# SyncE issues the value pages of the last two samples, and GpSimd's squares in the first layer's output projections stand between two weight splits

## The chip, the cores and the metric

The kernel runs on one core of a Trainium2 chip. Five engines run their own streams and wait for each other on semaphores: TensorE (matrix products), VectorE, ScalarE, GpSimd and SyncE, which here only issues transfers. The metric is the device time of one execution in microseconds; lower is better. Three runs of the kernel before gave 1976.70, 1977.17 and 1978.89 us, a median of 1977.17.

## The reference

One inference step of a decoder with two layers, for a prompt of 1024 tokens and for 8 samples of 8 new tokens each (64 tokens), with a width of 1024, in float32. All 1088 tokens share the weights. Cut to what matters here:

```python
# layer 0: gated MLP over chunks
u, v, z = split(rmsnorm(x) @ w_in_a, 3)
x = x + (u * spatial_mix(rmsnorm(v)) * silu(z)) @ w_out_a      # 2048 -> 1024
# layer 1: sparse attention, 8 query heads, 2 key/value heads of 128
q, k, v, iq, ik, iw, z = split(rmsnorm(x) @ w_in_b)
idx = top_k(indexer_scores(iq, iw, ik_all), 256)               # per query token
x = x + (softmax(q @ k_sel) @ v_sel * silu(z)) @ w_out_b       # k_sel, v_sel: chosen positions
# after each layer
x = x + sigmoid(rmsnorm(x) @ w_gate) * (p @ w_pe)
```

A sample attends to 1024 past positions. Their keys and values lie in pools of pages of 128 positions, and page_table names the 8 pages of each sample: for each sample 8 pages of keys and 8 of values, 128 KB each, have to be fetched by number.

## The kernel before

**Activations and weights.** Activations are kept transposed, with channels on the partitions: xT is 8 tiles of 128 channels by 1092 columns (64 sample tokens, 1024 prompt tokens, 4 of padding). Weights come in 177 units of 1024 x 128 (512 KB). Each matrix product in full precision is made of three products of rounded parts: hi x hi, hi x lo, lo x hi. So each unit goes through four steps, and with two buffers (par 0 and 1, in turn) for each: SyncE loads wraw (unit, L602), ScalarE rounds it to whi (split_hi, L429) once TensorE has used the unit two before, GpSimd computes wlo = wraw - whi (split_lo, L434), and TensorE waits for w_lo and runs the unit (gemm, L446); w_used counts the units that it has left.

**Output projections of the first layer.** The first layer runs over two token groups, one after the other: 576 columns, then 512. In a group, w_out_a makes 8 tiles of output channels, each of two units (half 0 and half 1). When TensorE leaves a tile, VectorE adds it to xT (L1423) and raises xup. GpSimd then adds the squares of that tile to acc (add_squares: the square L759, the sum L760), for the norm that follows; for tile 7 that is left to ScalarE. In the order of GpSimd's stream the squares of tile f stand right behind the two splits of turn f, which are unit 2f + 1 and unit 2f + 2 of the projection; the next turn's first split, of unit 2f + 3, is behind them. From tile 3 of the second group on, VectorE also makes the low parts that the gate needs (gate_lo, L493) right behind L1423.

**Sample attention.** It follows the prompt attention in the second layer. TensorE goes through the samples with a lead: for each b it transposes the probabilities of b (sample_turn), folds sample b - 1 (L2500), makes the logits of b + 2, transposes the keys of b + 3 (k_pages, L2442) and multiplies the probabilities of b with its values (sample_values: L2485 for the new tokens, L2489 for the pages). Key and value pages have three buffers each, kpg and vpg, taken in turn by b % 3. SyncE issues key pages (key_pages): those of samples 0 to 2 early, those of 3 to 7 when the keys of b - 3 have been transposed (sa["kt"]). GpSimd issues value pages: samples 0 to 2 during the prompt attention, then eight loads of z tiles, then samples 3 to 7, each when the product of sample b - 3 is done (sa["pv"]). Each issue (sample_pages, L589) reads a page number into a register and starts one transfer; the transfers of sample b raise vpin[b % 3], or kpin[b % 3] for keys, by 16 each. Behind its last value page GpSimd clears acc (L855) and makes the low part of unit 162, the second of w_out_b. Behind its last key page SyncE waits for the last sample's output and then reloads xT from DRAM (L713).

**Behind it.** VectorE copies the last sample out (L1894), multiplies it with the gate z (L1873), ScalarE rounds it (L1282), VectorE takes the low part (L1938), and TensorE starts the output projection of the second layer.

Of the kernel before, what the change touches and what calls it, by code (L numbers as in the profile page):

```python
# [28 lines left out]
KD = D // P  # L29
SEQ, DEC_B, DEC_T = 1024, 8, 8  # L30
# [7 lines left out]
KA = AW // P  # L38
# [4 lines left out]
PAGE, NPAGE = 128, 8  # L43
# [14 lines left out]
U_A = [0, 64]  # L58
# [5 lines left out]
def tile_cols(j):  # L64

    return (0, NS) if j == 0 else (NS + CHUNK * (j - 1), CHUNK)
# [52 lines left out]
def hybrid_trunk(nc, x_prompt, x_sample, cache_k, cache_v, cache_ik, page_table, p_prompt, p_sample,  # L119
# [5 lines left out]
    with ctx:  # L125
        def sem(name):
            return ctx.enter_context(nc.semaphore(name))
# [60 lines left out]
        sqa = rbc  # L188
# [83 lines left out]
        vpg = [pl(f"vpg{q}", [P, NPAGE, NKV * DH]) for q in range(2)]  # L272
        vpg = [[t[:, 0:NPAGE // 2], t[:, NPAGE // 2:]] for t in vpg]
# [67 lines left out]
        sA = [Turn(gmlp, {n: g * {"vsq": 5, "rv": 1, "xup": KD}.get(n, KA) for n in gmlp}) for g in range(2)]  # L341
# [50 lines left out]
        sa = {n: sem(f"sa_{n}") for n in ("pre", "qc", "kt", "ke", "s", "mx", "nb", "ex", "nr", "tr", "pt", "pv", "hd", "ft", "o")}  # L392
        kpin, vpin = ([sem(f"{n}{q}") for q in range(3)] for n in ("kpin", "vpin"))
# [10 lines left out]
        for n, (b, h) in enumerate(STEPS):  # L404
# [3 lines left out]
            PIECES += [(n, b, h, m) for m in range((b + 4) // 4)]  # L408
        SPREAD_AT = [FIRST[n] - 1 for n in SPREAD] + [len(PIECES)]
        LAST = [FIRST[n] + (b + 4) // 4 for n, (b, _) in enumerate(STEPS)]  # L410
        FRONT = ((2, 0), (3, 0))
        SCORES = ([(b, c, h) for b, c in FRONT for h in range(IH - 2)] +
# [18 lines left out]
        def split_lo(pool, par, u):  # L431

            pool.wait_ge(w_hi, u + 1)
            nc.gpsimd.tensor_tensor(wlo[par][:], wraw[par][:], whi[par][:].bitcast(F32),  # L434
                                    ALU.subtract).then_inc(w_lo, 1)
# [136 lines left out]
        def group_cols(g):  # L572
            c0, n, _, _, np_ = GROUPS[g]
            return [(c0 + n // np_ * m, n // np_) for m in range(np_)]
# [9 lines left out]
        def sample_pages(eng, dst, src, b, done, pages=range(NPAGE)):  # L584

            for g in pages:
                page = eng.value_load(ptab[0:1, b * NPAGE + g:b * NPAGE + g + 1],
                                      min_val=0, max_val=cache_k.shape[0] - 1)
                eng.dma_start(dst(g), src[bass.ds(page, 1), 0].rearrange("a s g d -> s (a g d)")).then_inc(done, 16)  # L589

        def value_pages(pool, b, pages=range(NPAGE)):
            if b >= 3:
                pool.wait_ge(sa["pv"], b - 2)
            sample_pages(pool, lambda g: vpg[b % 3][g // 4][:, g % 4, :], cache_v, b, vpin[b % 3], pages)

        @block.sync
        def _(sp):
# [14 lines left out]
            for j in range(9):  # L612
                c0, n = tile_cols(j)
# [87 lines left out]
            def key_pages(b):  # L701
                if b >= 3:
                    sp.wait_ge(sa["kt"], b - 2)
                sample_pages(sp, lambda g: kpg[b % 3][:, g, :], cache_k, b, kpin[b % 3])
# [4 lines left out]
                key_pages(b)  # L709
            for b in range(3, DEC_B):  # L710
                key_pages(b)
            sp.wait_ge(sa["o"], DEC_B)
            sp.dma_start(xT[:].rearrange("p f n -> p (f n)"), xs).then_inc(xs_in, 16)  # L713
            sp.wait_ge(oy["lo"], KD)
# [10 lines left out]
        def _(pool):  # L725
# [31 lines left out]
            def add_squares(sq, f, a, n):  # L757

                own.link(nc.gpsimd.tensor_tensor(sq, xT[:, f, a:a + n], xT[:, f, a:a + n], ALU.mult))  # L759
                own.link(nc.gpsimd.tensor_tensor(acc[:, a:a + n], acc[:, a:a + n], sq, ALU.add))  # L760

            for g in range(2):
                c0, n, _, _, np_ = GROUPS[g]
                for base, trips in ((U_A[g], KA // 2), (U_A[g] + KA, KA)):
                    with pool.Fori(0, trips) as i:
                        for ff in range(2):
                            split_lo(pool, (ff + 1) % 2, base + 2 * i + ff + 1)
                    if base == 0:
                        pool.wait_ge(ws_ev, 2)
                        own.link(nc.gpsimd.affine_select(out=wsT[:], in_=wsT[:], compare_op=ALU.is_ge, fill=0.0, base=0,  # L770
                                                         pattern=[[0, NGRP], [1, P]], channel_multiplier=-1))
                        for b in range(DEC_B):
                            t = slice(DEC_T * b, DEC_T * b + DEC_T)
                            pool.dma_start(wsbd[t, :, t], wsT[0:DEC_T, :, 0:DEC_T]).then_inc(bd_in, 16)
                pool.wait_ge(nA[g]["sum"], nA[g].at("sum", np_))
                own.link(nc.gpsimd.memset(acc[:, c0:c0 + n], 0.0))
                for f in range(KD):
                    for half in range(2):
                        split_lo(pool, (half + 1) % 2, U_A[g] + 3 * KA + 2 * f + half + 1)
                    if f < KD - 1:  # L780
                        pool.wait_ge(sA[g]["xup"], sA[g].at("xup", f + 3))
                        add_squares(sqa[:, c0:c0 + n], f, c0, n)
                pool.sem_inc(stat, 1)

            def gate_pool(layer, last):
# [53 lines left out]
            for i in range(NBLK * NKV):  # L839
                pool.wait_ge(at_["rs"], i + 1)  # L840
                if i:
                    pool.wait_ge(at_["tr"], SPREAD_AT[i - 1] + 1)
                nc.gpsimd.tensor_tensor(rdiag[:], ident[:].unsqueeze(1).broadcast_to((P, REP, P)),
                                        ars[:, REP * i:REP * i + REP].unsqueeze(2).broadcast_to((P, REP, P)),
                                        ALU.mult).then_inc(at_["dg"], 1)
                if 1 <= i <= 6:
                    value_pages(pool, (i - 1) // 2, range(4 * ((i - 1) % 2), 4 * ((i - 1) % 2) + 4))
# [2 lines left out]
                pool.wait_ge(z_st[q], 16 * (KD // 2))  # L850
            for f in range(KD):
                pool.dma_start(zb[f][:], zs[f]).then_inc(z_in[f // 2], 16)
            for b in range(3, DEC_B):
                value_pages(pool, b)
            own.link(nc.gpsimd.memset(acc[:], 0.0))  # L855
            for f in range(KD):
# [9 lines left out]
        def _(act):  # L866
# [349 lines left out]
            def pieces_out(n):  # L1216
                for i in range(FIRST[n], LAST[n]):
                    _, b, h, m = PIECES[i]
                    k = min(4, b + 1 - 4 * m)
                    act.wait_ge(at_["tr"], i + 1)  # L1220
                    if n >= REP:
                        act.wait_ge(at_["pv"], n // 2 - 1)
                    nc.scalar.activation(PTs[:, 4 * m:4 * m + k, h % REP, :],
                                         PS[:, 4 + i % 2, 0:k * P].rearrange("p (k q) -> p k q", q=P),
                                         ACT.Copy).then_inc(at_["pt"], 1)
# [726 lines left out]
        def _(pe):  # L1952
# [19 lines left out]
            for g in range(2):  # L1972
                c0, n, nch, has_s, np_ = GROUPS[g]
# [57 lines left out]
                with pe.Fori(0, KA // 2) as i:  # L2031
                    for ff in range(2):
                        f = 2 * i + ff
# [195 lines left out]
            for m, (b, c, h) in enumerate(SCORES):  # L2229
                n = min(BANK, (b + 1) * P - c * BANK)  # L2230
                p0 = ID * (h % 2)
                c0 = tile_cols(1 + b)[0]
# [244 lines left out]

            def sample_values(b):
                pe.wait_ge(sa["pt"], b + 1)
                pe.wait_ge(vpin[b % 3], 16 * NPAGE * (b // 3 + 1))  # L2480
                if b:
                    pe.wait_ge(sa["hd"], b)
                tiles = [(q, g, PS[NS * q + 32 * g:NS * q + 32 * g + 32, 3, 0:P]) for q in range(2) for g in range(NKV)]
                for g in range(NKV):
                    nc.tensor.matmul(tiles[g][2], PsT[0:NS, 8, 32 * g:32 * g + 32], vtok[0:NS, 0, g * DH:(g + 1) * DH],  # L2485
                                     start=True, stop=False)
                for j in range(NPAGE // 2):
                    for q, g, out in tiles:
                        mm = nc.tensor.matmul(out, PsT[:, 2 * j + q, 32 * g:32 * g + 32],  # L2489
                                              vpg[b % 3][q][:, j, g * DH:(g + 1) * DH], start=q == 1 and j == 0,  # L2490
                                              stop=j == NPAGE // 2 - 1)
                mm.then_inc(sa["pv"], 1)
# [15 lines left out]
            for b in range(DEC_B):  # L2508
                sample_turn(b)
                if b:  # L2510
                    fold_halves(b - 1)
                if b + 2 < DEC_B:
                    sample_logits(b + 2)
                if b + 3 < DEC_B:
                    k_pages(b + 3)
                sample_values(b)
# [32 lines left out]
```

## Time and profile before

| | |
|---|---|
| median of three runs | 1977.17 us (1976.70 to 1978.89) |
| span of the profiled execution | 1973.8 us |
| its own time | the page gives the span alone; the median of the runs is 3.4 us above it |
| TensorE busy | 1863.0 us, 94% |
| VectorE, ScalarE, GpSimd busy | 862.2, 793.2, 649.9 us |
| DMA | 150.76 MB, mean 76 GB/s |

A busy TensorE doesn't mean TensorE at its peak: its clock has two levels, 2.4 and 1.2 GHz, and PEclk in a row is the mean granted one as a share of the upper. Rows in order of time give the start in us from the start of the span, the duration, the engine and line, what is written and read, the count of instructions merged in the row, and in brackets how long the engine stood idle before and what ended that. "issue" stands for time in which the profile shows nothing that the engine waited for. POOL is GpSimd, DVE is VectorE, ACT is ScalarE, PE is TensorE, PEld its weight loads, SPq SyncE's issues.

### The profile page before, as it was taken

The page shows a single profiled execution, that of the slowest core. Times are in us where ns is not written, and L with a number is a line of the kernel's source. Part 1 is how long each engine was busy: PE and PEld are TensorE (multiplying, and loading weights), DVE is VectorE, ACT ScalarE, POOL GpSimd, SP SyncE. Part 2 cuts the span into 40 slices and gives each one's busy share as a digit, 9 for nine tenths or more (in the row PEclk, how much of TensorE's full clock was granted, in tenths as well). Part 3 has the DMA queues.
Part 4 walks back from the last instruction along what each step waited for, and adds up shares of the span by engine and source line. Part 5 has one row for each costly group of instructions (what it writes and reads, how often), then busy time and mean ns, then how long its engine had stood idle before and what let it go on. Part 6 is the DMA issues. An engine that isn't in the chain of part 4 may idle for free. (4 is left out here: it accounts for less than half of the span.)

```text
span 1973.8 us, 30722 instructions
## 1 busy us (share of the span) xinstructions
PE 1863.0 (94%) x11000; PEld 1647.2 (83%) x11000; DVE 862.2 (44%) x1653; ACT 793.2 (40%) x1148; POOL 649.9 (33%) x397
## 2 busy tenths in 40 slices
PE   7999999899999999999979989999989998699998
PEld 7999999899887888779969549999966765499997
DVE  4113333311114444033254877687778634512433
ACT  4233333212243333233235675567865554402211
POOL 4333323265333334654522131111132002354220
PEclk9999999999999999999989899999999999899999
DMA  6223222222222222331123110312231006531111
GB/s 187 75 65 85 74 74 74 64 77 83 85 85 85 85 85 86 95 109 33 32 64 122 31 56 22 89 43 66 88 121 31 1 1 209 186 99 43 44 55 45
DMA packets 226179, 150.76 MB, mean 76 GB/s; under 512 B 16754, under 2 KB 219250, under 8 KB 225714
## 3 DMA queue, kind: packets, MB, share of 16 engines
q1 hardware_dynamic: 210754, 125.78, 21.6%
q0 software_dynamic: 5152, 14.48, 2.4%
q10 hardware_dynamic: 10192, 9.46, 1.4%
q8 instruction: 46, 0.75, 0.2%
q14 instruction: 35, 0.29, 0.1%
HBM read 133.24 MB, written 16.43 MB: 76 GB/s over the span
## 5 line engine op out<-in xcount | busy, mean ns | idle before, releaser
L434 POOL TENSOR_TENSOR wlo<-wraw,whi 128x1024 fp32r<-128x1024 f32 x177 | 430.2, 2431 | 722.4 <-ACT whi L429 720.3
L446 PE MATMUL PS<-hhi_g,whi 128*128 128x288 f32 (+1 forms) x1152 | 324.0, 335 | 12.2 <-POOL wlo L434 7.2
L429 ACT ACTIVATE whi<-wraw 128x1024 fp32r<-128x1024 f32 x177 | 186.6, 1055 | 343.0 <-PE PS L446 324.6
L446 PE MATMUL PS<-hhi_g,wlo 128*128 128x288 f32 (+1 forms) x1152 | 317.1, 330 | 0.0
L446 PE MATMUL PS<-hlo_g,whi 128*128 128x288 f32 (+1 forms) x1152 | 316.9, 329 | 0.0
L446 PE MATMUL PS<-hhi,whi 128*128 128x364 f32 x1176 | 269.7, 338 | 12.8 <-DVE hlo L559 6.8
L446 PE MATMUL PS<-hlo,whi 128*128 128x364 f32 x1176 | 262.0, 331 | 0.0
L446 PE MATMUL PS<-hhi,wlo 128*128 128x364 f32 x1176 | 260.6, 330 | 0.0
L446 PEld LDWEIGHTS PS<-hhi_g,whi 128*128 128x128 f32 x1152 | 195.7, 189 | 31.1 <-issue 6.6
L446 PEld LDWEIGHTS PS<-hhi,whi 128*128 128x128 f32 x1176 | 204.0, 191 | 20.4 <-issue 13.9
L446 PEld LDWEIGHTS PS<-hhi_g,wlo 128*128 128x128 f32 x1152 | 196.4, 189 | 17.7
L446 PEld LDWEIGHTS PS<-hlo_g,whi 128*128 128x128 f32 x1152 | 196.9, 190 | 16.2
L446 PEld LDWEIGHTS PS<-hlo,whi 128*128 128x128 f32 x1176 | 206.5, 190 | 0.0
L446 PEld LDWEIGHTS PS<-hhi,wlo 128*128 128x128 f32 x1176 | 206.3, 190 | 0.0
L446 PE MATMUL PS<-yhi,whi 128*128 128x288 f32 (+1 forms) x384 | 108.0, 335 | 5.3 <-POOL wlo L434 4.7
L1387 DVE TENSOR_TENSOR t2a<-PS,szt 128x576 f32<-128x576 f32 (+1 forms) x32 | 23.2, 725 | 198.9 <-PE PS L446 198.3
L446 PE MATMUL PS<-yhi,wlo 128*128 128x288 f32 (+1 forms) x384 | 106.0, 330 | 0.0
L446 PE MATMUL PS<-ylo,whi 128*128 128x288 f32 (+1 forms) x384 | 105.3, 329 | 0.0
L1626 DVE TENSOR_SCALAR_CACHE_REDUCE acc<-sc,thr 128x384 bf16<-128x384 f32 (+1 forms) x124 | 100.7, 812 | 4.1
L1344 DVE COPY v_raw<-PS 128x512 f32 x32 | 22.1, 691 | 176.7 <-PE PS L1998 91.2
L988 ACT ACTIVATE sig<-hfb 128x1092 f32<-128x1092 f32 x16 | 17.9, 1118 | 174.7 <-DVE hfb L1441 174.5
L1423 DVE TENSOR_TENSOR xT<-PS,xT 128x576 f32<-128x576 f32 (+1 forms) x16 | 11.6, 725 | 168.0 <-PE PS L446 168.0
(392 smaller groups left out, 2726.4 us busy)
## 6 DMA issues: line engine op xcount, KB each, us to landing
wraw<-in_w_in_a_dram SPq DMA_DIRECT2D x96, 512.0 KB, 3.9
wraw<-in_w_out_a_dram SPq DMA_DIRECT2D x32, 512.0 KB, 4.0
wraw<-in_w_in_b_dram SPq DMA_DIRECT2D x25, 512.0 KB, 3.7
wraw<-in_w_pe_gate_dram SPq DMA_DIRECT2D x16, 512.0 KB, 4.2
kpg<-in_cache_k_dram SPq DMA_DIRECT2D x64, 128.0 KB, 2.8
vpg<-in_cache_v_dram POOLq DMA_DIRECT2D x64, 128.0 KB, 2.4
xs<-xT SPq DMA_DIRECT2D x1, 4368.0 KB, 12.6
xT<-xs SPq DMA_DIRECT2D x1, 4368.0 KB, 14.0
```

Of the source, the lines that this page charges most:

```text
L429: nc.scalar.activation(whi[par][:], wraw[par][:], ACT.Copy).then_inc(w_hi, 1)
L434: nc.gpsimd.tensor_tensor(wlo[par][:], wraw[par][:], whi[par][:].bitcast(F32), ALU.subtract).then_inc(w_lo, 1)
L446: mm = nc.tensor.matmul(o, w[par][:, k, :], r(k, c0, cn), start=first and i == 0 and n == 0, stop=last and i == KD - 1 and n == 2)
L988: nc.scalar.activation(sig[:], tg, ACT.Sigmoid).then_inc(s["sig"], 1)
L1344: vdst = nc.vector.tensor_copy(v_raw[:, bass.ds(f, 1), 0:4 * P].rearrange("p o n -> p (o n)"), PS[:, 4 + 2 * ff, :])
L1387: nc.vector.tensor_tensor(t2a[:, 0:n].rearrange("p (b n) -> p b n", b=np_), PS[:, 2:2 + np_, 0:h], szt[:, 0:n].rearrange("p (b n) -> p b n ...
L1423: nc.vector.tensor_tensor(x, PS[:, b:b + np_, 0:h], x, ALU.add).then_inc(s["xup"], 1)
L1626: own.link(nc.vector.tensor_scalar(vdmp[:, 0:(b + 1) * P], area(b), thr[:, b - 2:b - 1], None, ALU.is_lt, ALU.add, accum_out=cnt[:, b - 2: ...
```

## The change

Three things. The value pages of samples 6 and 7 are issued by SyncE, behind its last key pages, and no longer by GpSimd; each still waits for the product of sample b - 3. Their transfers raise a semaphore of the key pages (the one that the keys of sample b - 1 had used), so value_sem(b) tells both the issuer and TensorE which semaphore and which count it is. And in the output projections of the first layer the squares of tile f - 1 stand in GpSimd's stream between the two splits of turn f, where the squares of tile f stood behind both. The number of squares, splits and transfers is the same.

```diff
+        def value_sem(b):
+            if b < DEC_B - 2:
+                return vpin[b % 3], 16 * NPAGE * (b // 3 + 1)
+            q = (b - 1) % 3
+            return kpin[q], 16 * NPAGE * ((DEC_B - 1 - q) // 3 + 2)
-        def value_pages(pool, b, pages=range(NPAGE)):
+        def value_pages(eng, b, pages=range(NPAGE)):
             if b >= 3:
-                pool.wait_ge(sa["pv"], b - 2)
-            sample_pages(pool, lambda g: vpg[b % 3][g // 4][:, g % 4, :], cache_v, b, vpin[b % 3], pages)
+                eng.wait_ge(sa["pv"], b - 2)
+            sample_pages(eng, lambda g: vpg[b % 3][g // 4][:, g % 4, :], cache_v, b, value_sem(b)[0], pages)
...
             for b in range(3, DEC_B):
                 key_pages(b)
+            for b in range(DEC_B - 2, DEC_B):
+                value_pages(sp, b)
             sp.wait_ge(sa["o"], DEC_B)
...
                 for f in range(KD):
-                    for half in range(2):
-                        split_lo(pool, (half + 1) % 2, U_A[g] + 3 * KA + 2 * f + half + 1)
-                    if f < KD - 1:
-                        pool.wait_ge(sA[g]["xup"], sA[g].at("xup", f + 3))
-                        add_squares(sqa[:, c0:c0 + n], f, c0, n)
+                    split_lo(pool, 1, U_A[g] + 3 * KA + 2 * f + 1)
+                    if f:
+                        pool.wait_ge(sA[g]["xup"], sA[g].at("xup", f + 2))
+                        add_squares(sqa[:, c0:c0 + n], f - 1, c0, n)
+                    split_lo(pool, 0, U_A[g] + 3 * KA + 2 * f + 2)
...
-            for b in range(3, DEC_B):
+            for b in range(3, DEC_B - 2):
                 value_pages(pool, b)
...
-                pe.wait_ge(vpin[b % 3], 16 * NPAGE * (b // 3 + 1))
+                pe.wait_ge(*value_sem(b))
```

## Rows read from the trace of the kernel before

**Rows 1.** The page: busy time and share of the span.
```profile
PE 1863.0 (94%) x11000; PEld 1647.2 (83%) x11000; DVE 862.2 (44%) x1653; ACT 793.2 (40%) x1148; POOL 649.9 (33%) x397
```

**Rows 2.** Groups of TensorE, 376 to 486 and 776 to 884: busy, mean, idle before.
```profile
L446 PE MATMUL PS<-yhi,whi 128*128 128x288 f32 x256 | 56.5, 301 | 0.3
...
L446 PE MATMUL PS<-yhi,whi 128*128 128x512 f32 x128 | 51.5, 402 | 5.1 <-POOL wlo L434 4.7
```

**Rows 3.** TensorE in order of time, 1630 to 1730.
```profile
1636.25 1.97 PE L2442 MATMUL PS<-ident,kpg 128*128 128x128 f32 x16
...
1683.22 1.08 PE L2489 MATMUL PS<-vpg,PsT 128*32 128x128 f32 x32
...
1696.22 0.41 PE L2485 MATMUL PS<-vtok,PsT 64*32 64x128 f32 x4
...
1697.57 0.66 PE L2475 MATMUL PS<-ident,Ps 128*128 128x128 f32 x4
...
1702.52 0.41 PE L2485 MATMUL PS<-vtok,PsT 64*32 64x128 f32 x4 [3.26 <-issue]
...
1712.11 0.64 PE L2485 MATMUL PS<-vtok,PsT 64*32 64x128 f32 x4 [5.53 <-issue]
...
1715.02 0.69 PE L2500 MATMUL PS<-rsb 128*128 128x64 f32 x2 [0.41 <-DVE rsb L1890]
1718.92 1.25 PE L446 MATMUL PS<-hhi,whi 128*128 128x364 f32 x3 [3.21 <-DVE hlo L1938]
```

**Rows 4.** GpSimd's issues of value pages in order of time; landing, 1680 to 1711.
```profile
1690.63 0.54 POOL L589 DMA_DIRECT2D vpg<-in_cache_v_dram  x1 [0.61 <-issue]
...
1709.63 0.54 POOL L589 DMA_DIRECT2D vpg<-in_cache_v_dram  x1 [0.61 <-issue]
...
DMA to landing us min/median/max: 2.2/2.3/3.4
```

**Rows 5.** SyncE's issues in order of time; landing of key pages, 1674 to 1684.
```profile
1638.96 44.02 SPq L589 DMA_DIRECT2D kpg<-in_cache_k_dram  x40
1716.00 0.33 SPq L713 DMA_DIRECT2D xT<-xs  x1
...
DMA to landing us min/median/max: 2.8/3.1/3.9
```

**Rows 6.** All engines in order of time around the last sample.
```profile
1700.15 0.21 ACT L1271 ACTIVATE PsT<-PS 64x64 f32<-64x64 f32 x1
...
1710.16 1.03 POOL L855 MEMSET acc<- 128x1092 f32 x1
1711.27 2.34 POOL L434 TENSOR_TENSOR wlo<-wraw,whi 128x1024 fp32r<-128x1024 f32 x1
...
1716.01 0.36 DVE L1873 TENSOR_TENSOR qT<-qT,zb 128x64 f32<-128x64 f32 x2
```

**Rows 7.** Windows: busy per engine, granted clock, DMA share, GB/s.
```profile
core 0: us, PE busy (x) PEld busy (x) DVE busy (x) ACT busy (x) POOL busy (x), PEclk, DMA share, GB/s
1703.10:1706.50 3.40, 3.40 (x39) 2.50 (x31) 0.29 (x1) 0.39 (x1) 1.54 (x4) 0.52 0.40 102
...
1718.90:1723.50 4.60, 4.58 (x15) 4.60 (x16) 4.60 (x8) 3.87 (x4) 0.00 (x0) 0.51 1.07 463
```

**Rows 8.** Second group's output projection, in order of time, 782 to 880.
```profile
791.69 0.69 DVE L1423 TENSOR_TENSOR xT<-PS,xT 128x512 f32<-128x512 f32 x1 [6.18 <-PE PS L446]
...
792.47 1.04 POOL L759 TENSOR_TENSOR rbc<-xT 128x512 f32<-128x512 f32 x1 [2.78 <-DVE xT L1423]
793.58 1.29 POOL L760 TENSOR_TENSOR acc<-acc,rbc 128x512 f32<-128x512 f32 x1
...
826.52 0.69 DVE L1423 TENSOR_TENSOR xT<-PS,xT 128x512 f32<-128x512 f32 x1 [10.92 <-PE PS L446]
826.58 1.07 ACT L429 ACTIVATE whi<-wraw 128x1024 fp32r<-128x1024 f32 x1 [3.86 <-PE PS L446]
827.13 1.35 DVE L493 SCALAR_TENSOR_TENSOR hlo<-xT,gp,hhi 128x1092 fp32r<-128x1092 f32 x1
827.29 2.08 POOL L759 TENSOR_TENSOR rbc<-xT 128x512 f32<-128x512 f32 x1 [3.19 <-DVE xT L1423]
...
830.82 4.90 POOL L434 TENSOR_TENSOR wlo<-wraw,whi 128x1024 fp32r<-128x1024 f32 x2
...
877.04 0.69 DVE L1423 TENSOR_TENSOR xT<-PS,xT 128x512 f32<-128x512 f32 x1 [10.69 <-PE PS L446]
```

## The prediction, made before the result was known

> **What bounds the kernel now.** Five views, in this order. The page first: TensorE is busy for 1863.0 of the 1973.8 us of the span, and no other engine for half of it [rows 1], so a change pays only where TensorE waits or runs at its lower clock. Then the groups of instructions over the two output projections of the first layer: TensorE's matmuls there stand idle 0.3 us in the first token group and 5.1 us in the second, 4.7 of it put down to GpSimd's low parts (L434) [rows 2]. Then TensorE in order of time through the sample attention, where it waits 3.26 us and 5.53 us in front of the value products of samples 6 and 7 [rows 3]. Then GpSimd's and SyncE's issues in the same stretch: which queue is late [rows 4, 5]. Last, the windows, for the clock granted around these waits [rows 7].
>
> The profiled execution has a span of 1973.8 us; the median of the three runs is 1977.17, that is 3.4 more for what lies around the span. I work on the span and take the difference off the median. What this kernel's measurement can tell from no change is about 0.2%, 4 us.
>
> **Part one: value pages of samples 6 and 7 on SyncE.** GpSimd issues samples 3 to 7 in one row: the last page of sample 5 starts at 1690.63, the last of sample 7 at 1709.63, 16 pages later, 1.19 us each with the gaps; a page lands 2.3 us after its issue (median) [rows 4]. So sample 7 lands at about 1711.9, and TensorE starts on it at 1712.11. The waits follow from GpSimd's pace of issue.
>
> SyncE is not quicker: 40 key pages take 44.02 us from the first start to the last end, (44.02 - 0.33) / 39 = 1.12 us a page (the 0.33 is one issue, as in the row of its reload) [rows 5]. But it ends with the keys at 1682.98 and then stands idle until 1716.00. What gates the moved pages:
> - sample 6 overwrites the buffer of sample 3, whose product ends at 1683.22 + 1.08 = 1684.30 [rows 3]. From a release to SyncE's first issue take 0.74 us: the first transposes of keys end at 1636.25 + 1.97 = 1638.22, SyncE starts at 1638.96 [rows 3, 5]. First page 1685.04.
> - sample 7 waits for the product of sample 4, which lies about halfway between that of sample 3 and that of sample 5 (1696.22) [rows 3], near 1692; SyncE has its eight pages for sample 6 out only at 1694.0, so it doesn't wait.
> - 15 more pages: last issue 1685.04 + 15 x 1.12 = 1701.84. Landing took between 2.8 and 3.9 us on this queue while both queues were full, 2.2 at the shortest and 3.4 at the longest on GpSimd's [rows 4, 5]. By then only one queue issues, so I take 2.4: 1704.3 (1703.9 to 1705.7).
>
> Sample 6's pages land by 1696 and no longer count. Its product then waits for ScalarE's copy of the probabilities, which ends at 1700.15 + 0.21 = 1700.36 [rows 6]: it starts at 1700.45 and not at 1702.52. Sample 7 by computation: product 1.35 us at the full clock (1696.22 to 1697.57, where the next group of matmuls starts), transposes 0.9, ScalarE's copy 0.8: ready at 1703.5. The pages, at 1704.3, are the later of the two. Start moves from 1712.11 to 1704.3: **7.8 us** (6.4 to 8.2; computation alone would give 8.6).
>
> After it, before: 2.91 us from the start of the product to the fold (1715.02), at half clock; at the full one 1.42 for the product, 0.29 for the copy and 0.1 between make 1.8, and the fold itself saves 0.1: **1.2 us**, which falls to 0 if the clock is low there all the same. The granted clock was 0.52 in 1703.1 to 1706.5, right after the 3.26 us wait, and 0.51 in 1718.9 to 1723.5 [rows 7]. With the two waits down to about 1.2 us each I expect the first of these gone. The second follows the 3.2 us in which TensorE waits for the first hi and lo parts of the output projection [rows 3], and that wait stays. It costs, over those 4.6 us, about 2.1 (15 matmuls of 364 columns, which at the full clock take some 2.5). Between keeping all of it (0) and losing it whole (2.1) I take **0.5**.
>
> Removed from GpSimd: 16 issues; its memset of acc and its low part of unit 162 were at 1710.16 and 1711.27 [rows 6] and can now start at 1691.8 and once ScalarE has the high part. ScalarE makes that only after its last copy of probabilities, ending near 1703.6, plus 1.07: low part 1704.8 to 1707.2, beside VectorE's first product with the gate (L1873, two inputs in SBUF [rows 6]), due at 1706.8. In the second token group a GpSimd square went from 1.04 to 2.08 us beside VectorE's L493, which has two SBUF inputs as well [rows 8]. So a collision here may cost up to 0.4 us: **minus 0.4**. The Trainium skill ("SBUF — State Buffer", Who interferes with whom) calls this an exclusive lock between VectorE and GpSimd, held for the whole instruction by whoever starts first; by it the 0.4 is due in full, and without it nothing. The doubled square agrees with it.
>
> Behind SyncE's 16 issues stands the reload of x, released by the last sample output (1716.00 before) [rows 5]; the pages are out by 1702.2 and the release comes near 1706.8, so nothing is held up. All later work follows the same releases and moves along. Part one: 7.8 + 1.2 + 0.5 - 0.4 = **9.1 us**.
>
> **Part two: squares between the splits.** Call T the moment TensorE leaves a tile. Before, in the second group, GpSimd does at T + 0.77 the squares of that tile (1.04 and 1.29), and only then the low part that TensorE wants half a tile later. That just fits: three tiles from 791.69 to 826.52, 11.61 each. From tile 3 on VectorE puts L493 (1.35 us, from T + 0.6) in front, the square takes 2.08, the low part ends near T + 6.75, and TensorE wanted it at T + 5.8. Four tiles from 826.52 to 877.04 take 12.63 each [rows 8]. Lost: 4 x 1.02 = **4.1 us** (the 4.7 of [rows 2] counts the drained pipe too).
>
> After: ScalarE's high part at T + 0.06 takes 1.07, the low part starts at T + 1.2, is held by L493 until T + 1.96 and ends at T + 4.4, against T + 5.8 wanted: 1.4 to spare. Squares of the tile before: 2.5 us with gaps, to T + 6.9. The second high part starts when TensorE leaves the unit, T + 5.8, and ends at T + 6.9; its low part ends at T + 9.4, wanted at T + 11.6: 2.2 to spare. All four waits go; what is next is TensorE itself. In the first group (tiles of 13 us, squares of 576 columns) TensorE did not wait [rows 2] and will not: no gain. The last squares end before T + 6.9 of tile 7's turn, ahead of the sums of the gate. Nothing is added, the same 28 squares and sums run. Bounds: 0 to 4.7, and below nothing only by the last rival. Part two: 4.1.
>
> **Sum.** 9.1 + 4.1 = 13.2: span 1960.6, median **1964.0 us**.
>
> **Rivals.**
> 1. Layer one gives nothing: L493 and the longer collision keep the first low part past T + 5.8. For it: the square did double. Against: it needs 1.4 us more than the one L493. Then only 9.1: 1968.1.
> 2. The transfers set the landing, not the issue: moving them brings nothing there. Then 4.1 and part of the clock: 1972. For it: both queues feed the same engines, and landing was longer while both ran (2.8 to 3.9 us). Against: the DMA share was 0.40 in 1703 to 1706.5 [rows 7] while TensorE waited. The Trainium skill ("DMA: Bandwidth & Descriptors", Issuing engines are not separate DMA queues) says the same: issuing on several engines saves only the sequencer's time. Here that time, 1.19 us a page, is what the waits are made of.
> 3. SyncE starts late on sample 6 or issues at 1.3 us a page: the last page lands at 1707 to 1708, part one is 5.5: 1967.6.
> 4. The low clock at 1718.9 goes too, and all is as in the forecast: 1.6 more, 1962.4.
> 5. Slower: the squares, now in front of the second low part, make it late. They would have to end 2.3 us later than worked out (two doubled squares do not suffice), T + 9.2; from there each tile pays. At 1.5 us in each of 14 tiles 21 us are lost, the 4.1 not won: 1977.2 - 9.1 + 21 = 1989.
>
> **Chances.** Forecast 0.66, rival 1 0.12, rival 2 0.04, rival 3 0.08, rival 4 0.08, rival 5 0.02. The low clock comes in stretches of some 3.4 us and may fall otherwise elsewhere, a microsecond or two either way. Range: 1960.3 (rival 4 and a little) to 1968.6 (rivals 1 and 3). Faster by over 0.2% 0.95, within 0.2% 0.03, slower 0.02.
>
> **What will show it.** Right: the first product of sample 7 begins near 1704.3 less what was won before it (by then 4.1 us), with under 1.5 us of wait; tiles of 11.6 us throughout the second group; no wait of TensorE for L434 there; SyncE's 16 pages 1.12 us apart, the first right behind sample 3's product. Wrong: pages of SyncE that start long after that product or land over 3.5 us after issue; a second low part that ends after T + 11.6; a clock of 0.5 from the product of sample 6 on.

## The result, and the profile after

The changed kernel takes 1959.14 us (median of four runs, 1957.59 to 1960.88), the kernel before 1978.03 on the same chip (1976.70 to 1980.30): a ratio of 0.9906, 95% interval 0.9893 to 0.9919. That is 18.9 us won. The prediction said 13.2 and a range of 1960.3 to 1968.6, so it was too small by 5.7 us, and the time lies 1.2 us below the range. The span of the profiled execution fell from 1973.8 to 1957.1, by 16.7. Three parts can be read from the rows below, and they add up to 8.0 + 1.3 + 9.05 = 18.4 us.

The same instruction has another line number in each kernel: in the changed one the product with the new tokens is L2494 (L2485 before), the fold L2509 (L2500), the update of xT L1432 (L1423), the product with the gate L1882 (L1873).

TensorE in order of time through the last samples, after the change; these rows answer to [rows 3]:

```profile
1690.10 0.41 PE L2494 MATMUL PS<-vtok,PsT 64*32 64x128 f32 x4
...
1694.29 0.41 PE L2494 MATMUL PS<-vtok,PsT 64*32 64x128 f32 x4 [1.15 <-ACT PsT L1280]
...
1697.98 0.41 PE L2494 MATMUL PS<-vtok,PsT 64*32 64x128 f32 x4 [1.14 <-ACT PsT L1280]
...
1699.81 0.43 PE L2509 MATMUL PS<-rsb 128*128 128x64 f32 x2 [0.41 <-DVE rsb L1899]
1703.46 1.25 PE L446 MATMUL PS<-hhi,whi 128*128 128x364 f32 x3 [3.21 <-DVE hlo L1947]
```

From sample 5's product to sample 7's it was 1712.11 - 1696.22 = 15.89 us, and is 7.88: 8.0 won, where the prediction had 7.8. From there to the output projection it was 6.81 and is 5.48: 1.3 won, against 1.2 less 0.4. SyncE's issues, answering to [rows 5], and the landing of the last moved pages (issued after 1690, when GpSimd issues none):

```profile
1679.03 17.06 SPq L589 DMA_DIRECT2D vpg<-in_cache_v_dram  x16
1700.53 0.33 SPq L722 DMA_DIRECT2D xT<-xs  x1
...
DMA to landing us min/median/max: 2.0/2.1/2.7
```

They are (17.06 - 0.33) / 15 = 1.115 us apart (1.12 predicted). The first starts 0.87 behind the end of sample 3's product (1678.16) and 0.78 behind the end of the last key page, which is the gap that SyncE has between any two of these pages (1.115 - 0.33): it did not stand idle for the product, as it had been expected to. The last is issued at 1695.76 and with the median landing of 2.1 us arrives near 1697.9, just when TensorE starts. So it seems to be the page that sample 7's product waits for, though the row names ScalarE, whose copy had ended at 1697.21; the runs with split pages below bear it out.

The windows, answering to [rows 7]: in this trace the first low clock is gone, the second is still there.

```profile
core 0: us, PE busy (x) PEld busy (x) DVE busy (x) ACT busy (x) POOL busy (x), PEclk, DMA share, GB/s
1694.20:1699.80 5.60, 3.96 (x79) 2.76 (x79) 1.89 (x8) 1.68 (x4) 1.50 (x1) 1.00 0.24 70
1703.40:1708.00 4.60, 4.54 (x16) 4.58 (x17) 4.60 (x8) 3.85 (x4) 0.00 (x0) 0.55 1.11 479
```

And the second group's output projection, answering to [rows 8]:

```profile
794.84 0.69 DVE L1432 TENSOR_TENSOR xT<-PS,xT 128x512 f32<-128x512 f32 x1 [6.18 <-PE PS L446]
...
828.44 0.69 DVE L1432 TENSOR_TENSOR xT<-PS,xT 128x512 f32<-128x512 f32 x1 [10.51 <-PE PS L446]
...
829.64 3.01 POOL L434 TENSOR_TENSOR wlo<-wraw,whi 128x1024 fp32r<-128x1024 f32 x1 [3.15 <-ACT whi L429]
832.61 1.03 POOL L768 TENSOR_TENSOR rbc<-xT 128x512 f32<-128x512 f32 x1
833.72 1.29 POOL L769 TENSOR_TENSOR acc<-acc,rbc 128x512 f32<-128x512 f32 x1
...
835.30 2.40 POOL L434 TENSOR_TENSOR wlo<-wraw,whi 128x1024 fp32r<-128x1024 f32 x1 [0.29 <-ACT whi L429]
839.64 0.69 DVE L1432 TENSOR_TENSOR xT<-PS,xT 128x512 f32<-128x512 f32 x1 [9.25 <-PE PS L446]
...
873.24 0.69 DVE L1432 TENSOR_TENSOR xT<-PS,xT 128x512 f32<-128x512 f32 x1 [9.24 <-PE PS L446]
```

This is the surprise. With T = 828.44 the first low part ends at T + 4.2, the squares at T + 6.6, the second low part at T + 9.3: all as worked out (4.4, 6.9, 9.4). But the seven steps from tile to tile take (873.24 - 794.84) / 7 = 11.20 us each, not 11.61. The pace that I took for TensorE's own was itself a stalled one. In the first group they went from 12.99 to 12.69, where no gain was expected at all. The groups of [rows 2], read again after the change, have lost even the idle time of 0.3 us that the first group had:

```profile
L446 PE MATMUL PS<-yhi,whi 128*128 128x288 f32 x256 | 55.7, 300 | 0.0
...
L446 PE MATMUL PS<-yhi,whi 128*128 128x512 f32 x128 | 50.7, 396 | 0.0
```

Seven steps in each group: 2.1 + (877.04 - 791.69 - 78.40 = 6.95) = 9.05 us, where the prediction had 4.1.

One reading of the two traces must not be made: that of the first 390 us. There both kernels have the same instructions, and yet the first tile of the first group comes 4.0 us later after the change (397.31 against 393.31); the low clock took other stretches (in 15 to 35 us the granted clock was 0.67 against 0.83 before, in 140 to 165 it was 0.86 against 0.93). Such drifts are why the parts are read by distances inside one trace, and why the medians of the runs, and not the two spans, carry the sum.

### The profile page after: what moved, and what is told of

It reads as the page before. It is cut to its first block and busy times, and to the rows that moved or that the text cites. A ratio compares the mean times of both kernels' runs of the same rounds, so it can differ in the third digit from the quotient of the medians.

```text
span 1957.1 us, 30722 instructions
## 1 busy us (share of the span) xinstructions
PE 1856.8 (95%) x11000; PEld 1645.7 (84%) x11000; DVE 872.8 (45%) x1653; ACT 793.2 (41%) x1148; POOL 640.1 (33%) x381
## 5 line engine op out<-in xcount | busy, mean ns | idle before, releaser
L1432 DVE TENSOR_TENSOR xT<-PS,xT 128x576 f32<-128x576 f32 (+1 forms) x16 | 11.6, 724 | 148.3 <-PE PS L446 148.3
## 6 DMA issues: line engine op xcount, KB each, us to landing
xs<-xT SPq DMA_DIRECT2D x1, 4368.0 KB, 12.6
```

What stands on the lines that cost most here:

```text
L1432: nc.vector.tensor_tensor(x, PS[:, b:b + np_, 0:h], x, ALU.add).then_inc(s["xup"], 1)
```

## The experiments

**One half at a time.** First the new order of squares without the moved pages, then the moved pages without the new order, and the changed kernel again on the same chip (before: 1978.35).

```diff
 # squares_only: the kernel before, with this part of the change alone
...
+                    split_lo(pool, 1, U_A[g] + 3 * KA + 2 * f + 1)
+                    if f:
+                        pool.wait_ge(sA[g]["xup"], sA[g].at("xup", f + 2))
+                        add_squares(sqa[:, c0:c0 + n], f - 1, c0, n)
+                    split_lo(pool, 0, U_A[g] + 3 * KA + 2 * f + 2)
```

> Only the new order of the squares, value pages as before. Theory: in the old order the first split of every tile ends a little after TensorE leaves the unit, also where no wait shows, so the gain is in all 16 tiles: tiles of 12.69 us in the first group (12.99 before) and 11.20 us in all of the second (11.61 and 12.63 before), 9 to 10 us in all, ratio about 0.995. Rival, as the prediction had it: only the four shown waits go, 4.1 us, ratio about 0.998, tiles of 11.6 us in the second group and 12.99 in the first, and the rest of the surplus is in the pages or the clock.

> Only the value pages of samples 6 and 7 on SyncE, squares as before. Theory: the start of sample 7's product moves 8 us nearer to that of sample 5, and 1.3 us follow behind it, 9 to 11 us in all with what the clock gives, ratio 0.9945 to 0.9955; layer one's tiles stay at 12.99, 11.61 and 12.63 us. Rival: the pages carry the whole surplus and this alone gains about 15 us, ratio 0.9925.

> The changed kernel once more, on the chip of the other three, as their yardstick. Both theories: 0.9906 of the kernel before, within its interval. If squares and pages act in different places, its gain is the sum of those of the two halves, within 2 us.

The squares alone: 1968.95 us, ratio 0.9956 (0.9942 to 0.9969), 9.4 won. The pages alone: 1969.16, ratio 0.9953 (0.9939 to 0.9966), 9.2 won. Both: 1959.11, ratio 0.9902 (0.9887 to 0.9917), 19.2 won, against a sum of 18.6. So the halves add up, the pages are worth what was predicted (9.1) and the squares more than twice as much (4.1 predicted); each interval is some 2.7 us wide to either side, and even its lower end for the squares, 6.1 us, lies above 4.1. With the pages alone the tiles are as before:

```profile
830.49 0.69 DVE L1432 TENSOR_TENSOR xT<-PS,xT 128x512 f32<-128x512 f32 x1 [10.91 <-PE PS L446]
```

(the tile before it at 818.88, the next one at 843.11: 11.61 and 12.62). With the squares alone they are 11.20:

```profile
827.57 0.69 DVE L1423 TENSOR_TENSOR xT<-PS,xT 128x512 f32<-128x512 f32 x1 [10.51 <-PE PS L446]
...
838.77 0.69 DVE L1423 TENSOR_TENSOR xT<-PS,xT 128x512 f32<-128x512 f32 x1 [9.24 <-PE PS L446]
```

**Where the stall had been all the time.** TensorE and GpSimd in the kernel before, at the end of the first unit of tile 1 of the second group:

```profile
794.95 2.40 POOL L434 TENSOR_TENSOR wlo<-wraw,whi 128x1024 fp32r<-128x1024 f32 x1
...
796.40 0.39 PE L446 MATMUL PS<-yhi,whi 128*128 128x512 f32 x1
...
796.63 0.40 PE L446 MATMUL PS<-ylo,whi 128*128 128x512 f32 x1
...
796.86 0.39 PE L446 MATMUL PS<-yhi,wlo 128*128 128x512 f32 x1
...
797.40 0.19 PEld L446 LDWEIGHTS PS<-yhi,whi 128*128 128x128 f32 x1 [0.58 <-POOL wlo L434]
797.40 0.50 PE L446 MATMUL PS<-yhi,whi 128*128 128x512 f32 x1
...
797.74 0.39 PE L446 MATMUL PS<-ylo,whi 128*128 128x512 f32 x1
```

Matmuls start every 0.233 us, so the next was due at 797.09. The low part ends at 797.35, and it starts at 797.40, 0.31 late; the one behind it comes 0.34 later and not 0.23. A likely reason, not tested, is that the first weight load (0.19 us, starting with the late matmul) no longer overlaps a matmul. Together 0.41 us, just 11.61 less 11.20. The matmul's row names no wait. The matmul before it is drawn as 0.39 us long, longer than the distance of two starts, and covers half of the gap; what is left, from 797.25 to 797.40, has no bracket in the row. Three such remainders of 0.15 us are about what [rows 2] has over the four large waits, 5.1 against 4.7, and the 0.3 us of the first group is of the same kind. The row of the weight load has the wait by name: 0.58 for GpSimd's wlo. Also 48 matmuls x 0.2333 = 11.20 gives the floor from the spacing alone. The first group shows the same at 438.59 (low part ends) and 438.64 (weight load, waited 0.27).

**Is it the low part's end?** Three ways to let it end earlier, with the pages as before. The first two kernels leave squares out of the sums and were run once each (1966.53 and 1969.61 us against 1979.17); they are read by their rows alone.

```diff
 # half_squares
-                        add_squares(sqa[:, c0:c0 + n], f, c0, n)
+                        add_squares(sqa[:, c0:c0 + n // 2], f, c0, n // 2)
 # no_squares
+                        if f == KD - 1 and half:
+                            pool.wait_ge(sA[g]["xup"], sA[g].at("xup", KD + 1))
...
-                    if f < KD - 1:
-                        pool.wait_ge(sA[g]["xup"], sA[g].at("xup", f + 3))
-                        add_squares(sqa[:, c0:c0 + n], f, c0, n)
 # squares_late: both splits, then the squares of the tile before
+                    split_lo(pool, 1, U_A[g] + 3 * KA + 2 * f + 1)
                     if f < KD - 1:
+                        split_lo(pool, 0, U_A[g] + 3 * KA + 2 * f + 2)
+                    if f:
+                        pool.wait_ge(sA[g]["xup"], sA[g].at("xup", f + 2))
+                        add_squares(sqa[:, c0:c0 + n], f - 1, c0, n)
+                split_lo(pool, 0, U_A[g] + 4 * KA)
```

> The kernel before, but GpSimd squares only the first half of each group's columns in the first layer's output projections (the sums of half the columns are left out). Theory: what stalls every tile is that the first split ends 0.1 to 0.3 us after TensorE has left the unit; half squares end about 1.2 us earlier, so that the tiles fall to the floor of 12.69 us in the first group and 11.20 in the first tiles of the second; from tile 3 on, where L493 holds the square up, 11.20 to 11.4. Rival: the 0.30 and 0.41 us a tile above the floor are a cost of the turn from tile to tile, and stay: 12.99 and 11.61.

> The kernel before without GpSimd's squares in the first layer's output projections (they are left out of the sums), the splits in their old order, the last one behind the update of tile 6. Theory: the floor, 12.69 us a tile in the first group and 11.20 in all of the second, just what the new order of the squares has, so that the new order hides them whole. Rival: without them the tiles are faster than with the new order, and some of their cost is left in the changed kernel.

> The kernel before, but in turn f GpSimd does the squares of tile f - 1 behind both splits, where it did those of tile f (in turn 7 they stand ahead of the last split). So the squares never wait for VectorE's update and are over before TensorE leaves the tile. Theory: what counts is that no first split stands behind a wait for the update, not that the squares stand between the splits: tiles of 12.69 and 11.20 us, ratio as with the new order alone, 0.9956 or so. Rival: behind both splits the squares still run into the next first split, and the tiles stay above the floor.

Half squares: 12.69 in the first group, 11.20 in the first tiles of the second, so the surplus is no fixed cost of a turn. From tile 3 on, where L493 runs, the tiles take 11.68, more than the 11.2 to 11.4 that I expected: there the square still takes 1.66 us in place of 0.61.

```profile
816.91 0.61 POOL L759 TENSOR_TENSOR rbc<-xT 128x256 f32<-128x256 f32 x1 [2.78 <-DVE xT L1423]
...
828.11 1.66 POOL L759 TENSOR_TENSOR rbc<-xT 128x256 f32<-128x256 f32 x1 [2.77 <-DVE xT L1423]
```

Without squares: 12.69 and 11.20, the floor, and no less than with the new order, which therefore hides all of their cost. Squares behind both splits: 12.69 and 11.20 too, 1968.86 us, ratio 0.9948 (0.9932 to 0.9965), the same as with the squares between the splits. In that kernel the squares of a tile end 0.4 us after TensorE has left the next one (1.29 + 839.16 = 840.45 against 840.07), a little later than expected. That costs nothing: the first low part of the next turn waits for ScalarE's high part and starts only 0.89 us after them.

```profile
835.67 2.41 POOL L434 TENSOR_TENSOR wlo<-wraw,whi 128x1024 fp32r<-128x1024 f32 x1 [2.58 <-ACT whi L429]
838.02 1.06 POOL L759 TENSOR_TENSOR rbc<-xT 128x512 f32<-128x512 f32 x1
839.16 1.29 POOL L760 TENSOR_TENSOR acc<-acc,rbc 128x512 f32<-128x512 f32 x1
841.34 2.95 POOL L434 TENSOR_TENSOR wlo<-wraw,whi 128x1024 fp32r<-128x1024 f32 x1 [0.89 <-ACT whi L429]
```

So, for the two places tried, what counts is not where the squares stand but that the first split of a tile no longer stands behind work that waits for the tile just finished.

**The collision with VectorE.**

```diff
 # gate_lo_late: VectorE, the kernel before
-                        if g and f >= 3:
-                            gate_lo(dve, 0, f - 3)
...
-                for i in range(5 if layer == 0 else 0, KD):
+                for i in range(KD):
```

> The kernel before, but VectorE makes none of the gate's low parts (L493) during the second group's output projection; all eight stand at the gate's start. Theory (GpSimd's square is held up by L493, 1.04 us, and that is the difference between the tiles of 11.61 and of 12.63 us): all tiles of the second group take 11.61, squares 1.04 us throughout, and TensorE no longer waits 1.17 us four times; 4.1 us won, of which 1.5 to 3 are given back at the gate's start, where TensorE waits for the first low parts. Rival: the longer squares have another cause (x_lo's rounding on ScalarE, the longer stream), and tiles of 12.63 us stay.

All squares take 1.04 us, and the tiles of the second group 11.59, all of them: the difference between 11.6 and 12.6 was L493 in front of the square, as the prediction had it. TensorE waits 2.1 us at the gate's start in exchange:

```profile
877.61 0.74 PE L446 MATMUL PS<-hhi,whi 128*128 128x364 f32 x3 [2.14 <-DVE hlo L493]
```

The median is 1973.87, ratio 0.9971 (0.9958 to 0.9983), 5.3 won; the rows explain 4.2 - 2.1 = 2.1, and the interval reaches down to 3.4. What the rest is stays open; the mean granted clock of its trace is 0.975, as in the one before.

**Pages: whose are the last, and what do they hold up?** First, sample 6 back to GpSimd.

```diff
 # s7_on_sync, from the changed kernel
-            for b in range(DEC_B - 2, DEC_B):
+            for b in range(DEC_B - 1, DEC_B):
                 value_pages(sp, b)
```

> The changed kernel, but only sample 7's pages on SyncE; sample 6's stay with GpSimd. Theory: in the changed kernel sample 7's product waits for its last page, by some 0.7 us more than for ScalarE's copy; here SyncE starts on sample 7 as soon as sample 4's product is done and is through some 1 us earlier, while GpSimd has sample 6's pages out at the time at which they were out before (about 8 us behind sample 5's last), which is 2 us later than its product could start. So sample 6 loses 2 us and sample 7's product then follows it: 1 to 1.5 us slower than the changed kernel. Rival: the last page alone counts, and it is 0.7 us faster than the changed kernel.

1961.14 us against 1959.11 for the changed kernel on the same chip: 2.0 slower, where 1 to 1.5 was expected. Sample 6's product waits 4.04 us for its pages, sample 7's no longer for its own: it starts 0.06 behind ScalarE's copy.

```profile
1694.51 0.64 PE L2494 MATMUL PS<-vtok,PsT 64*32 64x128 f32 x4 [4.04 <-issue]
...
1699.09 0.41 PE L2494 MATMUL PS<-vtok,PsT 64*32 64x128 f32 x4 [0.30 <-ACT PsT L1280]
```

From sample 5's product to the output projection the rows have more than that: 1705.25 - 1687.43 = 17.82 us, against 1704.44 - 1690.88 = 13.56 in the changed kernel on the same chip, 4.3 longer. Sample 6's product comes 2.9 later and runs at the low clock (0.50 from 1694.5 to 1698.5), and VectorE's product with the gate takes 1.03 us and not 0.36, because it runs into GpSimd's low part:

```profile
1700.14 2.34 POOL L434 TENSOR_TENSOR wlo<-wraw,whi 128x1024 fp32r<-128x1024 f32 x1 [7.25 <-ACT whi L429]
...
1701.66 1.03 DVE L1882 TENSOR_TENSOR qT<-qT,zb 128x64 f32<-128x64 f32 x2
```

Sample 5's product itself stands 3.5 us earlier in this trace than in that one, so the two spans differ by 0.9 us only. Why the medians differ by 2.0 and the rows by 4.3 stays open.

Then sample 7's pages split, four on each queue, each half with its own semaphore, and the changed kernel beside it.

```diff
 # split7, from the changed kernel
-            for b in range(DEC_B - 2, DEC_B):
-                value_pages(sp, b)
+            value_pages(sp, DEC_B - 2)
+            value_pages(sp, DEC_B - 1, range(NPAGE // 2, NPAGE))
...
             for b in range(3, DEC_B - 2):
                 value_pages(pool, b)
+            value_pages(pool, DEC_B - 1, range(NPAGE // 2))
```

> The changed kernel, but the first four value pages of sample 7 are issued by GpSimd, which has been idle since sample 5's last page, and only the last four by SyncE. Theory: in the changed kernel sample 7's product starts when its last page lands, 0.4 to 0.8 us after ScalarE's copy of its probabilities; with four pages fewer in front of it the last page lands 4 us earlier and the product starts right behind the copy. So its start follows that of sample 6's by 3.0 to 3.2 us in place of 3.7 to 3.9: 0.6 us, not to be told in the time but in the trace. Rival: the copy alone sets the start (the profile names it), nothing moves.

> The changed kernel again, as the yardstick on this chip. Both theories: 0.990 of the kernel before; the distance of the products of samples 6 and 7 3.7 to 3.9 us as before.

The product of sample 7 now starts 0.06 behind the end of ScalarE's copy; in the changed kernel of the same chip 0.91 behind it. So the pages had been the later of the two. The copy and the product, in the split kernel and then in the changed one:

```profile
1694.99 0.20 ACT L1282 ACTIVATE PsT<-PS 64x64 f32<-64x64 f32 x1
1695.25 0.41 PE L2500 MATMUL PS<-vtok,PsT 64*32 64x128 f32 x4 [0.42 <-ACT PsT L1282]
...
1696.43 0.21 ACT L1280 ACTIVATE PsT<-PS 64x64 f32<-64x64 f32 x1
1697.55 0.41 PE L2494 MATMUL PS<-vtok,PsT 64*32 64x128 f32 x4 [1.29 <-ACT PsT L1280]
```

The distance of the products is 4.49 us all the same, and not 3.0 to 3.2: sample 6's product ran at the low clock in this execution (L2500, 0.60 and not 0.41; granted clock 0.53 from 1691.0 to 1694.5), behind a wait of 1.15 us only. So short waits do not keep the low clock away from these samples in every execution. In time: 1957.43 against 1958.59, ratios 0.9899 (0.9881 to 0.9916) and 0.9904 (0.9887 to 0.9920), not to be told apart. The trace of this kernel shows something else:

```profile
1696.29 2.34 POOL L434 TENSOR_TENSOR wlo<-wraw,whi 128x1024 fp32r<-128x1024 f32 x1 [7.44 <-ACT whi L429]
...
1697.81 1.04 DVE L1884 TENSOR_TENSOR qT<-qT,zb 128x64 f32<-128x64 f32 x2
...
1701.40 1.25 PE L446 MATMUL PS<-hhi,whi 128*128 128x364 f32 x3 [3.89 <-DVE hlo L1949]
```

VectorE's two products with the gate take 1.04 us and not 0.36 (answering to [rows 6]), since the first can't end before GpSimd's low part does at 1698.63. That is the collision for which the prediction took off 0.4. It is there in two traces, this one and that of the kernel with sample 7's pages alone on SyncE, and both times the low part ends 0.82 us after VectorE has started. In the changed kernel it just doesn't happen: there the low part ends at 1700.65 and VectorE starts at 1700.54, and an overlap of 0.1 leaves no mark (0.36). A version without it, ScalarE rounding the unit one copy earlier:

```diff
 # split7_hi_early, ScalarE
                 if b + 2 < DEC_B:
                     exponents(b + 2)
+                if b == DEC_B - 2:
+                    act.wait_ge(sa["pv"], DEC_B - 2)
+                    split_unit(U_O + 1)
-            act.wait_ge(sa["pv"], DEC_B - 2)
-            split_unit(U_O + 1)
```

> The kernel with sample 7's pages on both queues, and ScalarE rounds unit 162 (the second of w_out_b) before its last copy of probabilities and no longer behind it. Theory: in that kernel GpSimd's low part of the unit was still running when VectorE began the product of the last sample with its gate, two inputs in SBUF, and the pair of those products took 1.04 us against 0.36: TensorE waited 3.89 us in front of the output projection against 3.21. One copy earlier the low part ends before the product begins: pair 0.36, wait 3.21, 0.7 us won in the trace, in the time hardly to be told. Rival: GpSimd is not what held VectorE; 1.04 and 3.89 stay.

> The same kernel without that move, on the same chip. Theory: pair 1.04, wait 3.89 us again. Rival: the two numbers differ from run to run without cause, 0.36 and 3.21 here too.

With it: low part from 1694.63 to 1696.97, the pair at 1699.12 takes 0.36, TensorE waits 3.21, as expected.

```profile
1694.63 2.34 POOL L434 TENSOR_TENSOR wlo<-wraw,whi 128x1024 fp32r<-128x1024 f32 x1 [2.96 <-ACT whi L429]
...
1699.12 0.36 DVE L1884 TENSOR_TENSOR qT<-qT,zb 128x64 f32<-128x64 f32 x2
```

Its samples also ran at the full clock, and here the distance expected of the split pages is there, 1696.56 - 1693.59 = 2.97 us, against 3.7 to 3.9 in the three traces of the changed kernel:

```profile
1693.59 0.41 PE L2500 MATMUL PS<-vtok,PsT 64*32 64x128 f32 x4 [1.15 <-ACT PsT L1282]
...
1696.56 0.41 PE L2500 MATMUL PS<-vtok,PsT 64*32 64x128 f32 x4 [0.42 <-ACT PsT L1282]
```

Without that move the expectation failed on this chip: 0.36 and 3.21 as well. Here sample 7's product fell into a low clock (0.64 for its first matmuls), VectorE came at 1702.69, half a microsecond behind the end of the low part at 1702.19. That fits a collision which depends on who comes when, and so do the other traces: 1.03 and 1.04 us where the low part ended 0.82 after VectorE's start, 0.36 where it had ended or had 0.1 left. But the kernel with the move and the one without it did not differ on this chip, so as a test of the move it shows nothing. Times: 1958.05 and 1958.90 us, ratios 0.9889 (0.9872 to 0.9905) and 0.9895 (0.9878 to 0.9911). The version with the move has the lowest ratio of all; it beats the kernel before by 1.1% and can't be told from the changed kernel (0.9902 and 0.9904 on other chips, with intervals that overlap its own).

## Why the prediction was too small, step by step

- **Value pages, right.** Predicted, and measured in brackets: pace of SyncE 1.12 us (1.115), landing 2.4 us (2.1), pages later than ScalarE's copy (0.8 us, from the computation 0.8 predicted), start of sample 7 moved by 7.8 us (8.0). The start was to wait for sample 3's product and came at SyncE's own pace. The pages alone won 9.2 us, 9.1 predicted; the interval of that run is 2.7 us to either side, so the closeness is in part luck.
- **What follows the last product, right in size.** 1.2 us predicted for the full clock, less 0.4 for the collision; measured 1.3 with no collision. The collision was rightly named and mistaken in size: where it happened it cost 0.68 us (3.89 against 3.21), and in the changed kernel nothing. The low clock at the start of the output projection stayed (0.55 in 4.6 us against 0.51), so of the 0.5 taken for it some 0.2 were won, an estimate from 0.04 x 4.6. These two misses, +0.4 and -0.3, nearly cancel. The prediction also says that the low clock comes in stretches of some 3.4 us; its own [rows 7] have 0.51 over 4.6.
- **The squares' new order, right.** Each step of its timetable came within 0.3 us.
- **What the old order cost, wrong.** This is the step that failed: "That just fits: three tiles from 791.69 to 826.52, 11.61 each", and for the first group "TensorE did not wait [rows 2] and will not: no gain". I took the pace of the tiles without a shown wait for TensorE's own, and compared the low part's end (T + 5.66 in those tiles) with half of that pace (T + 5.8). TensorE's own is 5.60 us a unit. So the low part was late in every tile, by a few tenths, and those are 0.41 a tile in the second group, 0.30 in the first; in the four tiles with L493 the stall is 1.43 and not 1.02. The term was 4.1 and is 9.05 by the tiles, 9.4 by the runs of the squares alone. The idle time in [rows 2] has 4.7 us for the four large waits and hardly anything of the rest (0.4 in the second group, 0.3 in the first), and the bound "0 to 4.7" that I set from it was no bound.
- **The rivals.** 1 (nothing in layer one) is refuted by the tiles, 2 (the transfers set the landing) by the last pages' landing of 2.0 to 2.7 us, 3 (SyncE late) by the 1.115 us. The Trainium skill ("DMA: Bandwidth & Descriptors", Issuing engines are not separate DMA queues) says that issuing on several engines saves the sequencer's time alone. The trace agrees: what was saved is issue time, that of 16 pages. The Trainium skill calls that time usually small beside the transfer itself. Here the measurement differs: it was 1.115 us a page against 2.1 to landing, and it set the pace. The Trainium skill ("SBUF — State Buffer", Who interferes with whom) calls what VectorE and GpSimd share an exclusive lock. The traces agree in both directions: GpSimd's square and low part were held by L493 (1.04 to 2.08, 2.40 to 3.01), VectorE's product by GpSimd's low part (0.36 to 1.04, with the low part ending 0.82 into it). Rival 4 (the low clock at the output projection goes) didn't come: 0.55 in that trace, 0.50 to 0.66 over the same 4.6 us in the other kernels with moved pages. Rival 5 (second low part late) had 2 us to go and never came near.

## What to carry to other kernels

Before the pace of a loop is taken for the engine's own, count it out: matmuls a turn times the distance of two starts in the middle of a unit, at the same granted clock. If the loop is slower, look for a stall even where the idle column says next to nothing: here a matmul is drawn 0.39 us long with the next one due after 0.233, and that hid half of a gap of 0.31; the rows of the weight loads showed it. And in an in-order stream keep the work that waits for this turn's result out from between two turns: one turn later it was free here, in both places tried.

## What was not expected of the hardware

A late semaphore cost TensorE more than its lateness: 0.31 us late, 0.41 lost. The first weight load behind the wait (0.19 us), which nothing covers, is the likely reason. And TensorE's low clock falls elsewhere from one execution to the next in code that is the same (397.31 against 393.31 at the first tile); over the 14 profiled executions the mean granted clock was between 0.972 and 0.978, without following their times: the kernel before had 0.975 with a span of 1973.8 us, the squares alone 0.973 with 1965.4.
